# Branch gates projected between the steps of the first block's attention and kept in DRAM until the branch products

## The reference

```python
h = rmsnorm(x, norm_g)
q_lat, kv_lat, k_pe, c_b, c_c, c_u, q_mem, g_attn, g_conv, g_mem, r = split_cols(h @ w_in, IN_SIZES)
# 8 attention heads over 512 keys (q, k from q_lat, kv_lat, with rope), 4 memory heads over 256 keys
o_attn = blocked_bidirectional_attention(q, k, v) * silu(g_attn)
o_conv = c_b * centred_short_conv(c_c * c_u, conv_w, conv_b) * silu(g_conv)
o_mem = softmax(mq @ m_k.T * scale) @ m_v * silu(g_mem)
r_attn, r_conv, r_mem = split_cols(sigmoid(r + b_gate), (1024, 1024, 1024))
y = r_attn * (o_attn @ w_br_attn) + r_conv * (o_conv @ w_br_conv) + r_mem * (o_mem @ w_br_mem)
return x + y @ w_out
```

## Time and profile before

| what | us |
|---|---|
| median of 3 runs (2509.62 to 2518.6) | 2512.87 |
| the profiled execution | 2520.28 |
| its span, first to last instruction | 2518.5 |
| TensorE busy | 2341.7 (93%) |
| VectorE busy | 1253.9 (50%) |
| GpSimd busy | 1224.5 (49%) |
| ScalarE busy | 886.2 (35%) |

### The profile page before, as it was taken

The page is one execution under the profiler, slowest core; times in us unless marked ns, Lnnn a source line. Parts: engine busy times, 40 slices in busy tenths (PEclk is TensorE's granted clock), DMA queues, the critical chain, the costliest instruction groups (busy, mean ns, idle before and its releaser), DMA issues.

```text
span 2518.5 us, 29591 instructions
## 1 busy us (share of the span) xinstructions
PE 2341.7 (93%) x9671; PEld 1787.0 (71%) x9678; DVE 1253.9 (50%) x2348; ACT 886.2 (35%) x1385; POOL 1224.5 (49%) x793
## 2 busy tenths in 40 slices
PE   7888888899998899899988889999999999999997
PEld 5554445678874566568877777888888788888886
DVE  2445442242221145628776774222222588888886
ACT  3443443433332244433332222222222333333332
POOL 2221100245430222133688888888888465555553
PEclk9999999899999899999998999999999999999999
DMA  5543212123221111022365566666665799999995
GB/s 210 168 156 95 89 47 76 38 76 100 92 88 63 63 43 43 26 84 85 80 138 101 125 126 131 144 149 144 137 108 108 234 338 345 355 352 352 353 356 213
DMA packets 222366, 379.70 MB, mean 151 GB/s; under 512 B 76848, under 2 KB 152624, under 8 KB 222032
## 3 DMA queue, kind: packets, MB, share of 16 engines
q1 hardware_dynamic: 143952, 311.31, 37.9%
q0 software_dynamic: 78336, 67.45, 13.2%
...
## 4 chain that ended last, share of the span: by engine, by line
PE 59%; DVE 4%; issue 1%; ACT 1%; POOL 0%; DMA 0%; DVEq 0%; ACTq 0%; another core or an unknown queue 0%; POOLq 0%
PE bank L1149 26%; PE bank L1160 20%; PE bank L961 8%; PE bank L1090 2%; PE bank L1061 1%; DVE u_split L1723 1%; PE bank L1128 1%; DVE tail L1789 1%; DVE tail L1791 1%; DVE tail L1792 1%; PE bank L1074 1%; ACT u_split L1434 0%; PE bank L1013 0%; DVE tail L1735 0%; DVE staged L1738 0%
## 5 line engine op out<-in xcount | busy, mean ns | idle before, releaser
L836 POOL TENSOR_TENSOR u_split<-blocks,u_split 128x1024 fp32r<-128x1024 f32 x106 | 257.1, 2425 | 898.4 <-ACT u_split L1274 897.5
L896 POOL DMA_INDIRECT gates<-low x384 | 621.4, 1618 | 116.9 <-issue 116.9
L1149 PE MATMUL bank<-h_high,u_split 128*128 128x512 f32 x2048 | 641.2, 394 | 33.3 <-DVE u_split L1723 32.2
L961 PE MATMUL bank<-h_high,u_split 128*128 128x512 f32 (+1 forms) x1696 | 574.4, 410 | 23.4 <-DVE h_low L1580 12.2
L1160 PE MATMUL bank<-v_split,a_split 128*128 128x512 f32 x2304 | 522.7, 389 | 2.7 <-DVE a_split L1850 2.7
L1160 PEld LDWEIGHTS bank<-v_split,a_split 128*128 128x128 f32 x2304 | 432.4, 188 | 92.9 <-DVE v_split L1847 3.1
L1149 PEld LDWEIGHTS bank<-h_high,u_split 128*128 128x128 f32 x2048 | 390.3, 191 | 118.2 <-DVE u_split L1723 34.7
L961 PEld LDWEIGHTS bank<-h_high,u_split 128*128 128x128 f32 (+1 forms) x1696 | 326.6, 193 | 110.6 <-issue 24.9
L1149 PE MATMUL bank<-h_low,u_split 128*128 128x512 f32 x1024 | 403.1, 394 | 0.0
L1723 DVE TENSOR_TENSOR u_split<-tail,u_split 128x1024 fp32r<-128x1024 f32 x128 | 156.5, 1227 | 416.0 <-ACT u_split L1434 415.5
L961 PE MATMUL bank<-h_low,u_split 128*128 128x512 f32 x720 | 286.3, 398 | 0.0
...
## 6 DMA issues: line engine op xcount, KB each, us to landing
tail<-in_uT SPq DMA_DIRECT2D x128, 512.0 KB, 3.8
tail<-in_v SPq DMA_DIRECT2D x128, 512.0 KB, 5.6
...
tail<-gates SPq DMA_DIRECT2D x128, 192.0 KB, 5.5
...
```

The costliest lines, as they stand in the source:

```text
L836: nc.gpsimd.tensor_tensor(flat(u, 1)[:, 0:n], ring[:, loads[0] % NW, 0:n], flat(u, 0)[:, 0:n].bitcast(F32), ALU.subtract).then_inc(s_wlo, 1)
L896: nc.gpsimd.indirect_dma_start(gate_elements, bass.IndirectOffsetOnAxis(ap=expert_no[tb][:, k:k + 1], axis=0), expert_gate[tb][:, k:k + 1] ...
L961: last = mm(ps[0:m, :], flat(u, part)[:, k * m:(k + 1) * m], x, start=(k == 0 and j == 0), stop=(k == nk - 1 and j == 2))
L1149: last = mm(bank[slot % 2][:, :], U2[:, slot % 2, w, k, :], x[:, k, :], start=(k == 0 and x is hh and w == 0), stop=(k == KD - 1 and w == 1))
```

## The change

Six things are different.

1. `fill` now ends with the 24 `r` tiles (`branch_gate`) in place of the memory values, and there are four fillers per head instead of two: one behind the second value product, one between the value products and the scores of the next head, and two after `O`. Twelve `r` tiles (0 to 11) come to stand in heads 4 to 7.
2. The memory values are made in head 7, behind its second value product.
3. The scores of memory head 0 stand at the end of head 7, and those of each further memory head behind the value products of the one before it; both `gate` tiles of a head stand between its scores and its transposes.
4. Of the other twelve `r` tiles, one stands behind the last memory head and eleven behind the split of its outputs. Then the 24 `br` tiles follow one another.
5. An `r` tile is evacuated as a plain copy, and SyncE stores it to DRAM (`branch_gates`, 256 KB each) after the fifth weight load behind its own. In the branch stage SyncE reads it back into one of 8 slots (`rgate`, in the place of `hT` and `h_low`, which is free once the last `r` tile is done): the read-back of gate `j` stands behind the load of `br` tile `j + 2`, and waits for the product `rb` 8 before.
6. The sigmoid is a step of its own on ScalarE, in place in `rgate`, ahead of the evacuation of `br` tile `j`; VectorE's product takes `rgate` and the evacuated `br` tile.

The number of matmuls is the same. The diff:

```diff
--- before.py
+++ after.py
@@ -86,6 +86,7 @@
+KEPT_R = []
@@ -170,7 +171,12 @@
     fill += [lambda: (STEPS.append(("norm", "mem")), normed("qm", 0))]
     fill += [lambda h=h: normed("qm", h) for h in range(1, MEM_HEADS)]
     fill += [lambda h=h: normed("mk", h) for h in range(MEM_HEADS)]
-    fill += [mem_values]
+
+    def branch_gate(j):
+
+        KEPT_R.append(tile("r", j, KD, P, True))
+
+    fill += [lambda j=j: branch_gate(j) for j in range(3 * KD)]
 
     def filler():
         if fill:
@@ -218,19 +224,21 @@
         STEPS.append(("PV", h, 1))
         if h + 1 < HEADS:
             filler()
+        else:
+            mem_values()
         more()
         more()
         columns(h, 3)
         STEPS.append(("PV", h, 2))
         STEPS.append(("PV", h, 3))
         if h + 1 < HEADS:
-            rows(h + 1)
+            filler()
+        rows(h + 1)
         STEPS.append(("O", h))
         if h + 1 < HEADS:
             filler()
+            filler()
             STEPS.append(("W", h + 1, TB - 1))
-    while fill:
-        filler()
     def gate(i):
 
         n = tile("gate", i, KD, P, i < 4)
@@ -239,25 +247,27 @@
 
     for h in range(MEM_HEADS):
         a = HEADS + h
-        rows(a)
+        gate(2 * h)
+        gate(2 * h + 1)
         STEPS.append(("W", a, TB - 1))
-        gate(2 * h)
         if h >= 2:
             STEPS.append(("split", "b", 4 * (h - 2), 4 * (h - 1)))
         for kb in range(MB):
             columns(a, kb)
         for kb in range(MB):
             STEPS.append(("PV", a, kb))
+        if h + 1 < MEM_HEADS:
+            rows(a + 1)
         STEPS.append(("O", a))
-        gate(2 * h + 1)
+    filler()
     for i in range(4):
         post("mgate", i, [])
     STEPS.append(("split", "b", 8, 12))
-    for f in range(KD):
-        for b in range(3):
-            n1 = tile("r", 3 * f + b, KD, P, True)
-            n2 = tile("br", 3 * f + b, 4, P, True)
-            post("rb", 3 * f + b, [n1, n2])
+    while fill:
+        filler()
+    for j in range(3 * KD):
+        STEPS.append(("sigmoid", j))
+        post("rb", j, [tile("br", j, 4, P, True)])
     STEPS.append(("split", "y", 0, KD))
     for f in range(KD):
         post("res", f, [tile("wo", f, KD, P, True)])
@@ -491,6 +501,8 @@
         hl = place("h_low", 4096, [KD, T], F32R)
 
         B2 = [place("branch_weights0", lists_off, [2, 4 * P], F32R), place("branch_weights1", mkT_off, [2, 4 * P], F32R)]
+        NR = 8
+        rgate = region(4096, NR * T, NR)
         yl = place("y_low", R1, [KD, T], F32R)
         ol = place("o_low", oT_off, [12, T], F32R)
         oh = (place("o_high", HH + 4096, [8, T], F32R), place("o_high_mem", PT_off, [4, T], F32R))
@@ -515,6 +527,7 @@
+        raw_r = nc.dram_tensor("branch_gates", (3 * KD, P, T), F32, kind="Internal").ap()
@@ -534,6 +547,9 @@
+        s_rkept = [sem(f"branch_gate_stored_from{i}") for i in range(NE)]
+        s_rback = [sem(f"branch_gate_in_slot{i}") for i in range(NR)]
+        s_sig = sem("sigmoids_done")
@@ -646,6 +662,13 @@
 
 
 
+        kept_count, kept_in = {}, [0] * NE
+        for n in KEPT_R:
+            kept_in[TEMPS[n] % NE] += 1
+            kept_count[n] = kept_in[TEMPS[n] % NE]
+        temp_of = {j: n for n, j in TEMPS.items()}
+        last_x = max(n for n, p in enumerate(PROJ) if p[0] in ("lat", "kpe", "conv", "gate", "qm", "r"))
+
         slots, came_before, place_after = {}, {}, {}
         users = {True: [], False: []}
         for n, (kind, _, loads) in enumerate(PROJ):
@@ -728,9 +751,31 @@
                 sp.dma_start(gates[4 * c:4 * c + 4].rearrange("i p t -> p i t"),
                              zeros.rearrange("p (i t) -> p i t", i=4)).then_inc(s_zero, 16)
 
+            def keep_r(j):
+                n = KEPT_R[j]
+                slot = TEMPS[n] % NE
+                sp.wait_ge(s_evac, n + 1)
+                sp.dma_start(raw_r[j], ebuf[:, slot, :]).then_inc(s_rkept[slot], 16)
+
+            def r_back(j):
+                n = KEPT_R[j]
+                sp.wait_ge(s_rkept[TEMPS[n] % NE], 16 * kept_count[n])
+                if j < NR:
+                    sp.wait_ge(s_proj, last_x + 1)
+                else:
+                    sp.wait_ge(s_post, post_no[("rb", j - NR)])
+                sp.dma_start(rgate[:, j % NR, :], raw_r[j]).then_inc(s_rback[j % NR], 16)
+
+            r_load = {L: i for L, (kind, i, _) in enumerate(LOADS) if kind == "r"}
+            first_br = next(L for L, (kind, _, _) in enumerate(LOADS) if kind == "br")
+
             sp.wait_ge(s_zset, 1)
             for L in range(len(LOADS)):
                 weights(L)
+                if L - NW in r_load:
+                    keep_r(r_load[L - NW])
+                if 0 <= L - first_br - 2 < 3 * KD:
+                    r_back(L - first_br - 2)
                 if NW <= L < NW + NKEYS // 4:
                     zero_gates(L - NW)
                 if L == NW - 1:
@@ -1211,16 +1256,14 @@
                 if n in TEMPS:
                     j = TEMPS[n]
                     dst = ebuf[:, j % NE, :]
-                    if j >= NE:
+                    if j >= NE and temp_of[j - NE] in kept_count:
+                        act.wait_ge(s_rkept[j % NE], 16 * kept_count[temp_of[j - NE]])
+                    elif j >= NE:
                         act.wait_ge(s_post, POST_OF[j - NE])
                     if kind == "conv" and i == 0:
                         act.wait_ge(s_tab, 1)
-                    if kind == "r" and i == 0:
-                        act.wait_ge(s_par, 16)
                     if kind == "gate" or (kind == "conv" and i % 4 == 3):
                         A(dst, ps[:, :], ACT.Silu).then_inc(s_evac, 1)
-                    elif kind == "r":
-                        A(dst, ps[:, :], ACT.Sigmoid, bias=col("bg", i)).then_inc(s_evac, 1)
                     elif kind == "wf":
                         A(dst[0:8, :], ps[0:8, :], ACT.Identity, bias=col("bf", 0, 0, 8)).then_inc(s_evac, 1)
                     else:
@@ -1378,6 +1421,12 @@
                     evac(s[1])
                     for u in split_after.get(s[1], []):
                         high_weights(u)
+                elif s[0] == "sigmoid":
+                    j = s[1]
+                    act.wait_ge(s_rback[j % NR], 16 * (j // NR + 1))
+                    if j == 0:
+                        act.wait_ge(s_par, 16)
+                    A(rgate[:, j % NR, :], rgate[:, j % NR, :], ACT.Sigmoid, bias=col("bg", j)).then_inc(s_sig, 1)
                 elif s[0] == "sq":
                     squares(s[1])
                 elif s[0] == "square":
@@ -1668,10 +1717,12 @@
                     end(V.tensor_tensor(oT[:, 8 + i, :], oT[:, 8 + i, :], memgate[:, i, :], ALU.mult), s_post, "s_post")
                 elif kind == "rb":
                     f, b = i // 3, i % 3
+                    dve.wait_ge(s_sig, i + 1)
+                    r = rgate[:, i % NR, :]
                     if b == 0:
-                        end(V.tensor_tensor(yT[:, f, :], e[0], e[1], ALU.mult), s_post, "s_post")
+                        end(V.tensor_tensor(yT[:, f, :], r, e[0], ALU.mult), s_post, "s_post")
                     else:
-                        link(V.tensor_tensor(dtmp, e[0], e[1], ALU.mult))
+                        link(V.tensor_tensor(dtmp, r, e[0], ALU.mult))
                         end(V.tensor_tensor(yT[:, f, :], yT[:, f, :], dtmp, ALU.add), s_post, "s_post")
                     dve.wait_ge(s_post, post_no[("rb", i)])
                 elif kind in ("res", "res2"):
```

## The result

The changed kernel took 2481.76 us (median of 4 runs, 2477.22 to 2486.72) against 2511.24 us for the kernel before (4 runs, 2506.42 to 2518.6) beside it: ratio 0.9868, 95% interval 0.9846 to 0.989. Timed again later the changed kernel had the ratio 0.9876 (0.9848 to 0.9905), so what is to be explained is about -30 us (24 to 39 less, by the two intervals).

The account below looks back on a forecast made before the run. TensorE, busy 93% of the span, was taken as the bound, so only its waits and half-clock time could move. Idle -24.8, new idle +4.3 and +6.1, clock -11.0: -25.4 us, giving 2487.5 (written 2488), range 2473 to 2504.

Parts of the forecast that it names:

- -20.4 - 2.2 of idle: Attention: seven score waits behind the rope steps go (-20.4 us), and one of four transpose waits, head 7's (-2.2 us).
- -13.6 of clock: Attention: half-clock time returned with the removed gaps, 11.9 us for seven score gaps and 1.7 for one transpose gap.
- -1.2 at the transition: Into the branch stage: TensorE's 1.2 us wait at the first gate tile goes, since eleven tiles now follow one another.
- Forecast +6.1 us: Branch stage: new idle from separate product tiles, start-up, memset and late subtractions, +6.1 us with bounds 2 and 16.
- the memset's 0.6: Branch stage: GpSimd's 1.80 us memset now stands in its chain and leaves +0.6 us (0 to 1.8).
- chain of 3.03 us: Branch products: evacuation, cast and GpSimd subtraction take 3.03 us against 2.72 of cover, costing 3.4 us over 11 pairs.
- Rival 4: Branch stage: read-backs from DRAM set the pace, stage 37 us longer, 2524 us; chance 0.05.
- Rival 1: Branch stage: VectorE and GpSimd block one another, 7.6 us smaller gain, 2495 us; chance 0.17.
- Rival 3: Larger gain: the two tiles also hide three transposes, or the branch stage runs at its 2.72; 2475 us; chance 0.12.
- -1.0 + 4.3 + 2.6: Memory heads: head 8's value wait shortens (-1.0 us), new gap between gate tiles 0 and 1 (+4.3), its lost clock (+2.6).
- Rival 2: Remaining gaps keep or lengthen the stretches at 1.2 GHz, so clock is not given back; 2498 us; chance 0.14.
- 1.7 us per gap: Attention: 20.1 us of lost clock spread over twelve gaps of over 2 us, 1.7 us each.

Follow-up runs that it names:

- e1_mem_old: The changed kernel with the memory heads in the order of the kernel before: 2482.19 us, ratio 0.9866 to the kernel before.
- e2_branch_alone: The kernel before with only the branch stage changed (all 24 gate tiles ahead of it, through DRAM): 2518.59 us, ratio 1.0017 to the kernel before.
- e6_tile_moved: The changed kernel with each head's tile ahead of the scores moved behind O (fillers 1, 0, 3): 2521.7 us, ratio 1.0023 to the kernel before.
- the idle matmuls: Unused matmuls filling TensorE's waits: in e6_tile_moved 2500.39 us; in the kernel before 2503.85 us, with more of them 2499.72 us.
- e7_cast_first: The changed kernel with ScalarE's cast of the next branch weights ahead of the evacuation: 2481.07 us, ratio 0.9874 to the kernel before.

## Why the prediction was right, and where it was off

**Attention: right in the mechanism, and closer in the sum than in its parts.** Forecast -20.4 - 2.2 of idle and -13.6 of clock, -36.2 in all; measured -36.4 by the medians of e1_mem_old and e2_branch_alone, which differ in the attention stage and in where twelve gate tiles stand. (The -1.2 at the transition is won in e2_branch_alone already.) Idle fell by 20.7 us between the profiled executions of the two, not 22.6, because new waits came at the fourth score product; the medians then leave 15.7 us for the clock instead of 13.6 (the two executions themselves show 9.3 less busy time). That the two misses cancel to 0.2 us is luck. The rope waits went, the tile ahead of the scores is the cause (e6_tile_moved), and the idle matmuls show that the clock term is real and not a by-product of the moved work. Three transposes of 3.25 us stayed, as foretold.

**Branch stage: right.** Forecast +6.1 us with a stage of about 71 us from the first to the end of the last product tile; measured 75.4 - 3.1 = 72.3 us for 24 x 2.72 = 65.3 of matmuls, so +7.0. In time e2_branch_alone has +6.1 where the sum, with the transition, had +4.9. The 1.1 us for product 23 were 1.50, the memset's 0.6 was 0.56, and the chain of 3.03 us was the bound (e7_cast_first). Rival 4 had no ground: the read-backs land in 2.9 us, and the only sigmoid that waits longer for one is the second, 1.13 us, in the start-up for which the sum had 1.0. The table load stands before the first of them and in its landing time:

```profile
609.67 1.28 ACT L1234 ACT_TABLE_LOAD   x1
611.19 0.72 ACT L1234 ACTIVATE low<-low 128x512 f32<-128x512 f32 x1 [0.23 <-DMA low<-branch_gates]
```

```profile
low<-branch_gates SPq DMA_DIRECT2D x24, 256.0 KB, 2.9
```

Rival 1, the late second product of VectorE, did not occur either: GpSimd's subtraction took 1.45 us there, not 1.57 + 0.69. Rival 3 came to nothing: the three transpose waits stayed, and the stage did not run at 2.72 us per tile.

**Memory heads: the step that failed.** The sum had -1.0 + 4.3 + 2.6 = +5.9 us; measured about 0 (-0.4 by the medians, which come from two groups of runs, and are known to some 7 us). The new gap between the gate tiles was sized well (4.14 us for 4.28). But "the fourth score product still waits for the first exponential, as before: 8.4 us stay" was wrong. Three of these waits are 1.53 us instead of 2.39, 2.39 and 2.20, and the first is 0.25 instead of 1.41. Before, the scores came right behind a tile, and so its evacuation and a cast (494.71 to 496.24 on ScalarE for memory head 11), or its gate step on VectorE (469.49 to 470.1 for head 10), stood ahead of the first exponential's table load. Now the value products of the head before stand there, and the load starts 0.45 us after VectorE began on the maximum (501.25 behind 500.80). I followed the exponential's chain but not what is ahead of it in the queues. And I missed the price of two gate tiles in a row: in memory heads 8 and 9 the step of the second one stands ahead of `W` on VectorE (476.10 us, 0.69, right before `W` at 476.71), which makes two transposes wait 1.93 us, though I had named just this mechanism for the convolution steps. Net idle was +2.9 or +1.8 (against the two executions of the changed kernel) for a forecast +3.3, so here too errors of both signs nearly cancelled. The 2.6 us of clock that I added are to be seen right behind the new gap: the gate tile that follows it took 8.35 us in one execution and 7.26 in the other, at clocks of 0.66 and 0.77, where one at full clock takes 5.44. Over the whole stretch they don't show: the busy time of e1_mem_old (554.9 us to its first output tile) is that of the changed kernel in its second execution (554.4). What gave them back I can't say from these runs.

**A wait I did not foresee.** "In attention no such wait shows before" was no argument: two fourth score products in attention wait 2.69 and 0.56 us now. Before, the rope wait stood in that place: in e6_tile_moved, where it is back, the score products wait only in the memory heads again (4.8 us, 4 times, the longest 1.5).

**The clock.** -11.0 was the forecast net of clock; -18.6 and -8.1 were found in two executions of the changed kernel against the one of before, which at 2520.3 us was itself slower than the median, and 12.5 to 13.5 us are left for it by the medians. Rival 2 (the clock is not given back) falls by this and by e6_tile_moved, where 13.5 us of it are lost again. My even 1.7 us per gap was a mean over unlike gaps: more behind most score waits, nothing behind the one at 354.44.

**The sum.** By the parts it should have been -36.4 + 6.1 - 0.4 = -30.7, and -29.5 was measured, for a forecast of -25.4. The 4 to 5 us between them are the memory heads (6.3) less what the branch stage cost more (1.2), all of it within the spread of the runs.

The Trainium skill, page "SBUF — State Buffer", section "SBUF: two separate sides", states that a VectorE operation with two SBUF inputs and a GpSimd operation that reads SBUF exclude one another for the whole instruction; it was the ground for rival 1. The trace agrees: in e7_cast_first VectorE's product that begins at 636.35, inside GpSimd's subtraction of 635.74 + 1.29, ends 0.55 us after it, where the product alone takes 0.69. The rival that I made of the rule did not come true.
